# Placing SBUF tensors at 32-byte instead of 64-byte steps in a decoder-layer kernel

## Chip, cores and metric

The kernel runs on one core of a Trainium2 chip. The metric is the device time of one execution, in microseconds (us).

## What is computed

One decoder layer for 512 tokens of width 1024, and a final RMSNorm. In the reference's terms, cut:

```python
h = rmsnorm(x, norm1_g)
u_pool, q, k, v, qm, gate_logits = split(h @ w_in)
merged = (g0 * (pool_mixer(u_pool) @ w_branch_pool)      # causal pooling
        + g1 * (swa_with_sinks(q, k, v) @ w_branch_swa)  # window attention
        + g2 * (mem_attention(qm, mem) @ w_branch_mem))  # 256 memory tokens
x = x + merged @ w_out
h2 = rmsnorm(x, norm2_g)
# PEER: 8 heads pick 16 of 128*128 one-neuron experts per token
y = sum over picked experts of gate * gelu(h2 . u_e) * v_e
out = rmsnorm(x + y, final_norm_g)
```

## The kernel before

**Arithmetic.** TensorE works on fp32 data in three passes. Each operand is split into a high part (`_hi`, rounded to fp32r, a narrower float) and the remainder (`_lo`). A product is high times high, high times low and low times high, summed in PSUM.

**Weights.** All weights are one stream of 346 chunks of 128 x 1024 fp32 (512 KB). SP's queue loads a chunk into one of four `raw` buffers (line 264). ScalarE makes `w_hi` of it (line 761), GpSimd makes `w_lo` (line 415), both double-buffered, and TensorE uses the pair. TensorE reports `chunk_used`, on which ScalarE's next split waits.

**Stages.** In the projections, the expert scores and the gates of the branches, the weight chunk is the stationary operand and the moving one is `hT` (the normed tokens, transposed; line 438), a 128 x 512 operand. The branch projections take `yT` (branch outputs) as the moving operand instead (line 438 too). In the output projection and in the last stage, the values of the experts (line 635), the tokens are stationary (`mg` and `wT`, 128 x 128 at a time) and the weight chunk moves, 512 columns at a time. The stages follow each other: normalising and projecting (to about 280 us), gates and branches (to 500 us), output projection (to 519 us), queries and retrieval while expert scores run, then a stretch in which 64 expert chunks alternate with small bf16 matmuls on one-hot matrices `ohJ` and `ohI` (line 719, 907 to 1344 us), more expert scores, and from 1435 us on the value stage: 128 chunks of 24 matmuls. The last stage multiplies scores (`a_in`) by gates (`g_in`), both read back from HBM, into `wf` (VectorE, line 1356); ScalarE makes `wT_hi`, VectorE `wT_lo` (line 1360). Of `yT` there are 16 rows in a high and a low half, used for 8 output blocks. Of `mg` there are 8 rows, used for 4 token blocks and 2 column halves.

**Where the tensors lie.** One array `arena` of 212,800 bytes in each of the 128 partitions holds everything in SBUF. A `Place` hands out byte offsets in it in program order. The arena starts at byte 16,512 of a partition, which is 128 past a multiple of 512. `keep` holds what lives throughout: `x_sb`, `hT_hi`, `hT_lo`, `raw`, `w_hi`, `w_lo`, `subkeys`, `ident`, all of a multiple of 512 bytes each, and after them the small ones. Of those `gains` has 96 bytes, `pscale` 16, `sinks` 64, `freq` 8, `iota_b` 256, `iota_k` 64, `eps` 4, and eleven statistics arrays (`ssum` to `rinv`) 32 each. `front` is the offset after them. The other places start from it: `y` and `s`, then `a`, `g` and `p`, for the first half; `r`, and from `late` on `v`, for the second. Tensors of different stages share bytes. In these places the big tensors have multiples of 512 bytes; `gsm` has 128, and `ub`, `sA` and `sB` 2112 each.

```python
r = Place(front)
abuf = r("abuf", [2, T])
...
late = r.at
v = Place(late)
a_in = v("a_in", [4, T])
g_in = v("g_in", [2, BLOCKS, GROUP, STAGE_T])
wf = v("wf", [2, T])
wT_hi = v("wT_hi", [2, T], f32r)
wT_lo = v("wT_lo", [2, T], f32r)
```

Of the kernel before, what the change touches and what calls it, by code (L numbers as in the profile page):

```python
# [60 lines left out]
def build(nc, dram, out):  # L61
# [4 lines left out]
    with ExitStack() as ctx:  # L66
# [1 line left out]
        arena_size = 212800  # L68
        arena = ctx.enter_context(nc.sbuf_tensor("arena", [P, arena_size], mybir.dt.uint8))
        arena_at = int(nc.sbuf_base) - arena_size  # L70
        assert arena_at % 64 == 0

        class Place:

# [3 lines left out]
            def __call__(self, name, shape, dt=f32):  # L78
                t = nc.alloc_sbuf_tensor_at(name, [P] + list(shape), dt, offset=arena_at + self.at)
                size = int(np.prod(shape)) * (2 if dt == bf16 else 4)  # L80
                self.at += (size + 63) // 64 * 64
                assert self.at <= arena_size, (name, self.at)
                return t

# [1372 lines left out]
```

## Time and profile before

| | |
|---|---|
| median of 3 runs | 2138.91 us (2138.90 to 2138.99) |
| profiled execution, its own time | 2138.9 us |
| profiled execution, span of its instructions | 2137.1 us |
| TensorE busy | 2079.1 us, 97% of the span |
| VectorE, ScalarE, GpSimd busy | 57%, 37%, 40% |
| share of the 16 DMA engines, main queue | 45.0% |
| granted TensorE clock, mean | 0.988 of full |

The span runs from the first instruction to the last. The difference to the execution's own time, 1.8 us, lies around it. Busy times of matmuls overlap, since the profile gives each one from its start to a modelled end. So for TensorE the step from start to start is the cost of a matmul, and the timeline shows it.

### The profile page before, as it was taken

The numbers are of one execution on the slowest core, as the hardware profiler recorded it, in microseconds if no ns is written. First come the engines' busy times: TensorE is split into PE (matmuls) and PEld (weight loads), VectorE is DVE, ScalarE is ACT, GpSimd is POOL, SyncE is SP. The second block draws the span as 40 slices with busy tenths as digits, with TensorE's granted clock in tenths as the row PEclk, the third lists the DMA queues.
The fourth block names the chain that finished last, engine by engine and source line by source line (L and its number), as shares of the span: only waits on it lengthen the run. The fifth ranks groups of instructions, "written<-read, shape, count | busy, mean of one in ns | idle before, by whom it ended". The sixth has DMA issues, their size and how long they took to land.

```text
span 2137.1 us, 30302 instructions
## 1 busy us (share of the span) xinstructions
PE 2079.1 (97%) x10616; PEld 1712.0 (80%) x10616; DVE 1225.2 (57%) x1851; ACT 792.6 (37%) x1136; POOL 849.9 (40%) x361
## 2 busy tenths in 40 slices
PE   6979899999999999999999999999999999999998
PEld 5756788887888888888888888888888888888886
DVE  6688311113119999777777777015555555555556
ACT  5576422323223222355445544332222222222223
POOL 4411144444335544433333333444444444444443
PEclk9999999999999999999999999999999999999999
DMA  5211022222224545435665665665555555555552
GB/s 207 91 38 40 30 91 97 98 94 84 77 82 125 147 147 147 138 118 191 196 196 186 192 196 196 212 208 221 185 186 191 218 181 181 186 216 196 182 181 104
DMA packets 108516, 323.47 MB, mean 151 GB/s; under 512 B 11200, under 2 KB 11200, under 8 KB 106304
## 3 DMA queue, kind: packets, MB, share of 16 engines
q1 hardware_dynamic: 108192, 322.49, 45.0%
q10 hardware_dynamic: 288, 0.54, 0.1%
q8 instruction: 18, 0.29, 0.1%
q14 instruction: 18, 0.15, 0.0%
HBM read 253.78 MB, written 69.21 MB: 151 GB/s over the span
## 4 chain that ended last, share of the span: by engine, by line
issue 48%; PE 32%; POOL 19%; DMA 0%; POOLq 0%; DVE 0%; ACT 0%; SPq 0%
PE bank L635 32%; POOL w_lo L415 19%; DMA a_in<-a_rows 0%; POOLq L414 0%; DVE x_sb L1382 0%; POOLq L418 0%; DVE x_sb L1377 0%; POOL mask L401 0%; POOL mask L399 0%; DVE wf L1356 0%; DVE wT_lo L1360 0%; ACT wT_hi L992 0%; POOL mask L396 0%; POOL mask L404 0%; SPq L264 0%
## 5 line engine op out<-in xcount | busy, mean ns | idle before, releaser
L415 POOL TENSOR_TENSOR w_lo<-raw,w_hi 128x1024 fp32r<-128x1024 f32 x346 | 846.3, 2446 | 1268.4 <-ACT w_hi L761 1268.4
L761 ACT ACTIVATE w_hi<-raw 128x1024 fp32r<-128x1024 f32 x346 | 366.7, 1060 | 1219.4 <-PE bank L438 702.2
L438 PE MATMUL bank<-hT_hi,w_hi 128*128 128x512 f32 x1488 | 590.7, 397 | 0.8 <-POOL w_lo L415 0.4
L438 PE MATMUL bank<-hT_hi,w_lo 128*128 128x512 f32 x1488 | 580.3, 390 | 0.0
L438 PE MATMUL bank<-hT_lo,w_hi 128*128 128x512 f32 x1488 | 579.2, 389 | 0.0
L1360 DVE TENSOR_TENSOR wT_lo<-wf,wT_hi 128x512 fp32r<-128x512 f32 x128 | 313.1, 2446 | 131.2 <-ACT wT_hi L992 131.2
L438 PEld LDWEIGHTS bank<-hT_hi,w_lo 128*128 128x128 f32 x1488 | 279.3, 188 | 60.0
L438 PEld LDWEIGHTS bank<-hT_hi,w_hi 128*128 128x128 f32 x1488 | 279.6, 188 | 59.2 <-issue 4.1
L438 PEld LDWEIGHTS bank<-hT_lo,w_hi 128*128 128x128 f32 x1488 | 279.9, 188 | 56.0 <-issue 0.7
L635 PE MATMUL bank<-w_hi,wT_hi 128*128 128x512 f32 x1024 | 315.3, 389 | 0.1
L635 PE MATMUL bank<-w_lo,wT_hi 128*128 128x512 f32 x1024 | 315.2, 389 | 0.0
L635 PE MATMUL bank<-w_hi,wT_lo 128*128 128x512 f32 x1024 | 315.2, 389 | 0.0
L1356 DVE TENSOR_TENSOR wf<-a_in,g_in 128x512 f32<-128x512 f32 x128 | 89.1, 696 | 252.8 <-PE bank L635 160.6
L635 PEld LDWEIGHTS bank<-w_hi,wT_hi 128*128 128x128 f32 x1024 | 192.1, 188 | 40.4 <-DVE wT_lo L1360 0.6
L635 PEld LDWEIGHTS bank<-w_lo,wT_hi 128*128 128x128 f32 x1024 | 192.2, 188 | 39.9
L635 PEld LDWEIGHTS bank<-w_hi,wT_lo 128*128 128x128 f32 x1024 | 192.2, 188 | 39.9
L1334 DVE TENSOR_TENSOR ohJ<-iota_b,J 128x1024 bf16<-128x1024 bf16 x64 | 164.3, 2567 | 96.2 <-PE bank L719 96.2
L983 ACT ACTIVATE gstage<-bank 128x512 f32<-128x512 f32 x128 | 129.7, 1123 | 0.0
L1337 DVE TENSOR_TENSOR ohI<-eqI,G 128x1024 bf16<-128x1024 bf16 x192 | 121.4, 687 | 9.2
L1203 DVE TENSOR_TENSOR part<-sg,bank 128x512 f32<-128x512 f32 x24 | 15.1, 683 | 174.4 <-PE bank L438 174.4
L719 PEld LDWEIGHTS bank<-ohI,ohJ 128*128 128x128 bf16 x1536 | 85.9, 98 | 16.7 <-issue 16.7
L719 PE MATMUL bank<-ohI,ohJ 128*128 128x128 bf16 x1536 | 96.9, 219 | 0.0
(217 smaller groups left out, 1530.0 us busy)
## 6 DMA issues: line engine op xcount, KB each, us to landing
raw<-stream SPq DMA_DIRECT2D x346, 512.0 KB, 3.5
a_rows<-abuf SPq DMA_DIRECT2D x128, 256.0 KB, 4.0
g_rows<-gstage SPq DMA_DIRECT2D x32, 1024.0 KB, 6.1
g_in<-g_rows SPq DMA_DIRECT2D x16, 2048.0 KB, 9.4
a_in<-a_rows SPq DMA_DIRECT2D x128, 256.0 KB, 3.5
x_sb<-x SPq DMA_DIRECT2D x4, 512.0 KB, 8.9
out<-x_sb SPq DMA_DIRECT2D x4, 512.0 KB, 2.7
subkeys<-subkeys SPq DMA_DIRECT2D x1, 1024.0 KB, 14.2
```

The costliest lines, as they stand in the source:

```text
L415: pool.tensor_tensor(w_lo[:, k % 2, :], raw[:, k % RAW, :], w_hi[:, k % 2, :].bitcast(f32), ALU.subtract).then_inc(lo_ready, 1)
L438: last = pe.matmul(dst, w[:, slot, k * P:(k + 1) * P], rhs[low][:, r0 + k - k0, :], start=(k == k0 and wi == 0), stop=(k == k1 - 1 and wi ...
L635: last = pe.matmul(bank[2 * t + half][:, :], lhs[low_l][:, t * P:(t + 1) * P], w[:, slot, half * 512:(half + 1) * 512], start=first and lo ...
L719: last = pe.matmul(bank[2 + b][:, tk * P:(tk + 1) * P], ohJ[:, di, at, :], ohI[:, di, q, at, :], start=(q == 0), stop=(q == 2))
L761: act.activation(w_hi[:, base % 2, :], raw[:, slot, :], ACT.Copy).then_inc(hi_ready, 1)
L983: act.activation(gstage[:, half, :, t0:t0 + TOK_I // 2].rearrange("p i t -> p t i"), bank[2 + b][:, :].rearrange("p (t i) -> p t i", i=NKEYS),
L1203: dve.tensor_tensor(part[:, q, :], sg[:, q, :], bank[b][:, :], ALU.mult).then_inc(branch_read, 1)
L1334: dve.tensor_tensor(ohJ[:, di, :, :].rearrange(wide, e=2), ramp, over_keys(J2[:, toks, :]), ALU.is_equal)
L1337: last = dve.tensor_tensor(ohI[:, di, q, :, :].rearrange(wide, e=2), eqI[:, di, :, :].rearrange(wide, e=2), over_keys(G2[:, q, toks, :]), ...
L1356: dve.tensor_tensor(wf[:, di % 2, :].rearrange(tiles, b=BLOCKS), a_in[:, di % 4, :].rearrange(tiles, b=BLOCKS), g_in[:, di // GROUP, :, di ...
L1360: dve.tensor_tensor(wT_lo[:, di % 2, :], wf[:, di % 2, :], wT_hi[:, di % 2, :].bitcast(f32), ALU.subtract).then_inc(weighted_lo, 1)
```

## The change

Each tensor's size is rounded up to a multiple of 32 bytes instead of 64 before the next one is placed. The assertion on the arena's own start is relaxed likewise; the start itself stays where it is. No instruction, loop, semaphore or transfer is added, removed or reordered.

```diff
-        assert arena_at % 64 == 0
+        assert arena_at % 32 == 0
...
-                self.at += (size + 63) // 64 * 64
+                self.at += (size + 31) // 32 * 32
```

## Rows read from the trace of the kernel before

**Rows 1.** The page's first part: busy time, share of the span, instructions.

```profile
PE 2079.1 (97%) x10616; PEld 1712.0 (80%) x10616; DVE 1225.2 (57%) x1851; ACT 792.6 (37%) x1136; POOL 849.9 (40%) x361
```

**Rows 2.** Windows: from:to, length, busy us by engine, PEclk, DMA share, GB/s.

```profile
962.00:1344.00 382.00, 382.00 (x2672) 317.68 (x2671) 278.34 (x271) 192.83 (x223) 133.44 (x56) 1.00 0.59 191
1454.00:2110.00 656.00, 656.00 (x2896) 543.17 (x2894) 381.45 (x241) 190.04 (x240) 290.04 (x121) 1.00 0.53 188
```

**Rows 3.** The same view, TensorE alone, a stretch early in the kernel.

```profile
45.20:46.40 1.20, 1.20 (x4) 0.50 0.00 0
```

**Rows 4.** Groups by line and shape: busy us, mean ns of one, idle before.

```profile
L438 PE MATMUL bank<-hT_hi,w_lo 128*128 128x512 f32 x1488 | 580.3, 390 | 0.0
...
L635 PE MATMUL bank<-w_hi,wT_lo 128*128 128x512 f32 x1024 | 315.2, 389 | 0.0
...
L635 PEld LDWEIGHTS bank<-w_hi,wT_lo 128*128 128x128 f32 x1024 | 192.2, 188 | 39.9
...
L1337 DVE TENSOR_TENSOR ohI<-eqI,G 128x1024 bf16<-128x1024 bf16 x192 | 121.4, 687 | 9.2
...
L438 PE MATMUL bank<-yT_hi,w_lo 128*128 128x512 f32 x128 | 50.6, 395 | 0.0
...
L635 PE MATMUL bank<-w_hi,mg_hi 128*128 128x512 f32 x64 | 20.2, 395 | 0.0
```

**Rows 5.** Timeline, TensorE, value stage: start us, us; first and last of 13.

```profile
1599.32 0.61 PE L635 MATMUL bank<-w_hi,wT_hi 128*128 128x512 f32 x2
...
1604.76 0.61 PE L635 MATMUL bank<-w_hi,wT_hi 128*128 128x512 f32 x2
```

**Rows 6.** Timeline, TensorE, branch projection going over to a gate projection.

```profile
340.07 0.40 PE L438 MATMUL bank<-yT_hi,w_hi 128*128 128x512 f32 x1
...
342.87 0.39 PE L438 MATMUL bank<-hT_hi,w_hi 128*128 128x512 f32 x1
...
345.61 0.39 PE L438 MATMUL bank<-hT_hi,w_hi 128*128 128x512 f32 x1
...
346.97 0.39 PE L438 MATMUL bank<-hT_hi,w_hi 128*128 128x512 f32 x1
```

**Rows 7.** Timeline, TensorE, output projection; first and last of four pairs.

```profile
505.70 0.63 PE L635 MATMUL bank<-w_hi,mg_hi 128*128 128x512 f32 x2
...
507.10 0.63 PE L635 MATMUL bank<-w_hi,mg_hi 128*128 128x512 f32 x2
```

**Rows 8.** Timeline, TensorE, early stretch; first and last of four.

```profile
45.23 0.63 PE L492 MATMUL bank<-w_lo,memT_hi 128*128 128x512 f32 x1
...
46.51 0.47 PE L492 MATMUL bank<-w_lo,memT_hi 128*128 128x512 f32 x1
```

**Rows 9.** Timeline, TensorE, expert chunk behind bf16 matmuls; first and last of ten.

```profile
1012.50 0.39 PE L438 MATMUL bank<-hT_lo,w_hi 128*128 128x512 f32 x1
...
1014.59 0.39 PE L438 MATMUL bank<-hT_lo,w_hi 128*128 128x512 f32 x1
```

**Rows 10.** One line's instructions: count, ns min/median/max, first and last start.

```profile
L1108 DVE TENSOR_TENSOR sA<-sB x4: 691/692/693, 79.3 to 93.9; 128x512 f32<-128x512 f32 x4
```

**Rows 11.** The same view by tile: what touches `top`.

```profile
L1248 DVE MAX8 top<-cand x64: 274/280/298, 641.0 to 821.6; 128x8 f32<-128x128 f32 x64
...
L1255 DVE MAX8 top<-cand x64: 273/276/297, 652.8 to 833.4; 128x8 f32<-128x128 f32 x64
```

**Rows 12.** The same view by tile: what touches `ohJ`.

```profile
L719 PE MATMUL bank<-ohI,ohJ x1536: 219/219/230, 907.5 to 1343.0; 128*128 128x128 bf16 x192
```

**Rows 13.** Waits from 1400 us on: total us, times, longest.

```profile
DVE wf L1356 <- PE bank L635: 160.6, 118, 1.9
...
DVE wf L1356 <- DMA a_in<-a_rows: 92.2, 8, 77.3
```

**Rows 14.** The chain that ended last, around 1440 us: start, us, what.

```profile
1439.87 10.27 DMA a_in<-a_rows
...
1452.31 674.87 PE bank L635 x2976
```

## The prediction

> **What bounds the kernel now.** I read the first part of the page, then the windows: TensorE is busy for 97% of the span [rows 1], and in the long stretches all of the time, 656 of 656 us in the value stage and 382 of 382 in the gate stretch, at full clock [rows 2]. The chain that ended last is TensorE alone for its last 675 us [rows 14]. So the time is the number of matmuls times the step from one start to the next, and whatever the change does elsewhere counts only if it stretches those steps or opens gaps. VectorE has room in the value stage: it waits for TensorE 118 times, 1.36 us on average [rows 13].
>
> The groups by shape then show something that bears on placement: matmuls of one shape don't all last alike. Those on `hT` and `wT` take 389 to 390 ns, those on `yT` and `mg` 395 [rows 4]. Those are modelled ends, so I read starts. In the value stage 24 matmuls take 1604.76 − 1599.32 = 5.44 us, 226.7 ns each [rows 5]. On `yT`, 12 take 342.87 − 340.07 = 2.80 us, 233.3 each; on `hT` soon after, 6 take 346.97 − 345.61 = 1.36 us, 226.7 each [rows 6]. On `mg`, 6 take 1.40 us, 233.3 [rows 7].
>
> **What the change moves.** Fifteen small tensors lose 32 bytes each in `keep`: `gains` (96 instead of 128), `pscale`, `freq`, `eps` and the eleven statistics (32 instead of 64). `front` falls by 15 × 32 = 480 bytes. In what follows it every size is a multiple of 64 already, so all of it shifts by the same 480. The tensors before `gains` stay. Places modulo 512, from the arena's start and the sizes in the kernel's description:
>
> - `hT`, `raw`, `w_hi`, `w_lo`, `ident`: 128, unchanged.
> - `yT`, `mg`, `memT`, `abuf` (at `front` or whole multiples of 512 behind it): before 0, now −480, that is 32.
> - `ohJ`, `ohI`, `a_in`, `g_in`, `wf`, `wT` (128 further, for `gsm`): before 128, now 160.
>
> So the two operands of a matmul lie like this. `hT` with `w`: 128 and 128 before and after. `wT` with `w`: 128 and 128 before, 160 and 128 now. `yT` or `mg` with `w`: 0 and 128 before, 32 and 128 now.
>
> **Cost by part.**
>
> Instructions, transfers, waits: none added or removed, 0.
>
> TensorE on `hT`: unchanged, 0. It is the largest share (3 × 1488 of 10616).
>
> TensorE on `wT`: 3 × 1024 = 3072 matmuls, nothing covers them, and each ns of step costs 3.07 us. Before, the two kinds of pair that share their place modulo 512 ran at 226.7, the two that differ by 128 bytes at 233.3. That is a correlation over two distances (0 and 128), and no row has a distance of 32. From above the nearest row is 233.3: 3072 × 6.6 ns = +20.3 us. From below it is the stretch at half clock (granted 0.50, 1.2 GHz) [rows 3]: 3 matmuls of this shape take 46.51 − 45.23 = 1.28 us, 427 ns each [rows 8]. Half of that, 213.3 ns, would be a step at 2.4 GHz without anything extra: 3072 × −13.4 = −41.2 us. In between, a linear share 32/128 of 6.6 ns is 1.65 ns or +5.1 us. I take 0: the modulus is the nearest to the one seen fast, and in the expert chunks the step comes back to 226.7 from 232.2 after a break (1014.59 − 1012.50 over 9 matmuls, operands at the same places) [rows 9]. So that step is something that the stream settles into, and I expect 32 bytes not to push it out.
>
> TensorE on `yT` (3 × 128), `mg` (3 × 64) and 48 on `memT` as the stationary operand: 624 matmuls at 233.3, whose distance falls from 128 to 96. No row has 96. If they fell to 226.7: 624 × 6.6 = −4.1 us. If they rose as much again, +4.1. I take 0.
>
> TensorE on one-hots: 1536 small matmuls, both operands move together, 0. From the first to the last of 64 passes go 1343.0 − 907.5 = 435.5 us [rows 12], 6.91 for each of 63, of which 24 expert matmuls take 5.44 and 24 small ones the rest, 61 ns each. At 3% more (233.3 over 226.7) that would be 2.8 us.
>
> The Trainium skill (TensorE: Matmul & The Clock Gate, Back-to-back issue gap) puts a warm step of 512 columns at N/2.4 + 2.5 = 215.8 ns, and says nothing of the operands' addresses. The trace does not agree, 226.7 at best. By that page's figure the value stage would have an estimated 3072 × 10.9 = 33 us to give back, if new places freed it from the extra.
>
> Weight loads of `wT`: 188 ns [rows 4] under a step of 226.7, so 38.7 ns of cover. If a row of 128 values at an odd place took an eighth longer, 212 ns, it would still be covered. By more than a fifth it would show.
>
> VectorE and ScalarE: `sA <- sB` reads its source shifted by 4 to 32 bytes against the destination (shifts of 2 to 16 tokens are built from steps of 1, 2, 4 and 8 fp32 values) and takes 692 ns, 691 to 693 [rows 10]: the shift does not show in it. MAX8 writes its first eight values at a multiple of 64 from the tensor's start and the second eight 32 bytes on, at 280 and 276 ns [rows 11]. I take 0 for all of VectorE; the two engines are not on the path anyway. What it costs if that is wrong for bf16 stands under the rivals.
>
> Transfers: `abuf`, `a_in`, `g_in`, `gstage` move by 32 bytes modulo 512; chunk loads don't. The value stage uses 0.53 of the DMA engines [rows 2]. One transfer is on the path: at 1439.87 an `a_in` block lands after 10.27 us and VectorE, ScalarE and TensorE follow at 1452.31 [rows 14]. A 32-byte piece more in a row of 2048 bytes, 1 in 64, makes that 0.16 us. I take 0, at most +0.2.
>
> The Trainium skill (DMA: Bandwidth & Descriptors, How a descriptor splits into AXI transactions) says that a transfer is cut at multiples of 256 bytes and that a start off such a multiple costs extra beats of 32. No row here shows beats. By it the moved tensors, at 128 modulo 256 or 0 before, would read one beat more per row, an estimated 65 for 64: the same 0.16 us.
>
> Sum: the profiled execution's 2138.9 us (span 2137.1 and 1.8 around it) + 0 = 2138.9, and the median of the runs is 2138.91.
>
> **Rivals.**
>
> *The value stage takes the slower step.* Decides at: the `wT` and `w` operands no longer at the same place modulo 512. For it: both pairs at unlike places are slow, both at like ones fast, whether the tokens move (`yT`) or stand (`mg`). Against it: 128 bytes are four times 32. Price +20.3: 2159.2 us. A weaker form at the linear share gives 2144.0.
>
> *The value stage gets faster.* The step of 226.7 holds 13.4 ns more than half of the cold one, so there is something to lose. Against it: no row at full clock is near 213. Half of it back: −20.6, 2118.3 us.
>
> *Branch and output projections fall to 226.7 and nothing else moves*: 2134.8 us.
>
> *VectorE's bf16 operations lose a fast form.* `ohI` takes 687 ns for 1024 elements [rows 4], fp32 692 for 512 [rows 10]. At one element's pace that would be 1384, so four operations in a pass (`eqI`, three `ohI`) get 2.8 us longer. The window of 382 us holds 55.3 passes of 6.91 us, and VectorE is idle for (382 − 278.34)/55.3 = 1.87 us of each [rows 2]. Exposed 0.9 × 64 = 58 us: 2197. Against it: 160 is still a multiple of 32, and shifts of 4 bytes cost fp32 nothing.
>
> **How the numbers follow.** Under 0.2% (4.3 us) a measurement of this kernel hardly tells from no change. Nothing moves: 0.38. Only the branch and output projections fall (2134.8, still within 0.2%): 0.08. Value stage at 233.3: 0.25; at the linear share: 0.08. bf16 form lost: 0.05. Value stage faster: 0.16, spread down to 2097. Together: faster 0.16, same 0.46, slower 0.38. The likeliest is no change, 2138.9, its own range 2134.8 to 2140. The range over the cases: below 2128 lies some 0.10, above 2161 some 0.08, so 2128 to 2161.
>
> **What would show it.** Right: timeline rows of the value stage with 24 matmuls in 5.44 us, `yT` and `mg` at 233.3, `hT` at 226.7, the groups' means of `L635` and `L1337` at 389 and 687 ns, the wait for `a_in` at 10.3 us. Wrong: `wT` matmuls at 395 ns mean and 5.60 us per chunk, or 5.2 and below; VectorE's `ohI` over 1 us with TensorE waiting for it; a weight load over 188 ns. What would make it wrong is that two read streams of TensorE disturb each other by their distance, and that 32 bytes of distance are enough.

## The result and the profile after

The changed kernel takes 2159.01 us (median of 4 runs, 2158.59 to 2160.14) where the kernel before takes 2138.9. The ratio is 1.0099, 95% interval 1.0087 to 1.0110: slower by 20 us. The forecast was no change, 2138.9. The measured time is inside the stated range, and within 0.2 us of the first rival's 2159.2.

The instructions are the same 30302, and TensorE is still busy for 97% of the span. The page's first part, of after:

```profile
span 2158.0 us, 30302 instructions
...
PE 2096.3 (97%) x10616; PEld 1709.1 (79%) x10616; DVE 1226.7 (57%) x1851; ACT 792.1 (37%) x1136; POOL 850.9 (39%) x361
```

The instructions that touch `wT_hi` show where the time went: of one kind of value-stage matmul, the duration and the starts of the first and last. First before, then after.

```profile
L635 PE MATMUL bank<-w_hi,wT_hi x1024: 389/389/497, 1430.2 to 2125.9; 128*128 128x512 f32 x171
```

```profile
L635 PE MATMUL bank<-w_hi,wT_hi x1024: 392/395/504, 1430.9 to 2146.8; 128*128 128x512 f32 x171
```

The last starts 695.7 us behind the first before and 715.9 after: +20.2. Up to the first, the kernel has lost 0.7 us in the profiled pair. There are 3067 steps between the two, so 226.8 ns a step before and 233.4 after. TensorE is hardly idle in between: one spot has steps of 534 and 335 ns before and of 358 and 342 after. What comes after the stage takes the same 10.3 us in both.

The timeline of after, TensorE, in the value stage, answers to [rows 5]:

```profile
1596.32 0.63 PE L635 MATMUL bank<-w_hi,wT_hi 128*128 128x512 f32 x2
...
1601.92 0.63 PE L635 MATMUL bank<-w_hi,wT_hi 128*128 128x512 f32 x2
```

That is 24 matmuls in 5.60 us, 233.3 ns each, where it was 5.44 us. The branch projection and the gate projection behind it, to be set beside [rows 6]:

```profile
337.94 0.39 PE L438 MATMUL bank<-yT_hi,w_hi 128*128 128x512 f32 x1
...
342.16 0.39 PE L438 MATMUL bank<-hT_hi,w_hi 128*128 128x512 f32 x1
...
344.92 0.39 PE L438 MATMUL bank<-hT_hi,w_hi 128*128 128x512 f32 x1
...
347.64 0.39 PE L438 MATMUL bank<-hT_hi,w_hi 128*128 128x512 f32 x1
```

On `yT` 18 matmuls take 4.22 us, 234.4 ns each (233.3 before). The first 12 on `hT` behind them take 2.76 us, 230.0 each, as the stream settles (2.74 before); the next 12 take 2.72 us, 226.7 each, as before. The output projection, beside [rows 7]:

```profile
500.26 0.63 PE L635 MATMUL bank<-w_lo,mg_hi 128*128 128x512 f32 x2
...
503.06 0.63 PE L635 MATMUL bank<-w_lo,mg_hi 128*128 128x512 f32 x2
```

That is 12 matmuls in 2.80 us, 233.3 ns each, unchanged. (By its first and last matmul this stage runs from 480.5 to 525 us in the kernel before, and the value stage starts at 1430.2; the description of the stages puts them at 500 to 519 and at 1435.) The groups by shape and the single lines of after that answer to [rows 4, 10 to 12]:

```profile
L635 PE MATMUL bank<-w_hi,wT_lo 128*128 128x512 f32 x1024 | 321.3, 396 | 0.0
L635 PEld LDWEIGHTS bank<-w_hi,wT_lo 128*128 128x128 f32 x1024 | 192.5, 188 | 46.4
L1337 DVE TENSOR_TENSOR ohI<-eqI,G 128x1024 bf16<-128x1024 bf16 x192 | 121.3, 686 | 9.2
...
L1108 DVE TENSOR_TENSOR sA<-sB x4: 691/691/694, 79.5 to 94.1; 128x512 f32<-128x512 f32 x4
...
L1255 DVE MAX8 top<-cand x64: 274/276/296, 653.0 to 833.6; 128x8 f32<-128x128 f32 x64
...
L719 PE MATMUL bank<-ohI,ohJ x1536: 219/219/229, 907.7 to 1343.7; 128*128 128x128 bf16 x192
```

VectorE's operations, the weight loads and the one-hot matmuls last what they did. The matmuls on `wT` are longer, 396 ns instead of 389; those on `yT` are longer by 1 ns a step, and all others are as they were.

Other engines are not what slows these matmuls. The windows view of after, all engines, with the starts of TensorE in that stretch:

```profile
1793.85:1795.25 1.40, 1.40 (x8) 1.13 (x7) 0.00 (x0) 0.00 (x0) 0.00 (x0) 1.00 0.63 129
```

```profile
1793.72 0.63 PE L635 MATMUL bank<-w_hi,wT_hi 128*128 128x512 f32 x2
...
1795.12 0.63 PE L635 MATMUL bank<-w_hi,wT_hi 128*128 128x512 f32 x2
```

VectorE, ScalarE and GpSimd do nothing there, and 6 matmuls still take 1.40 us, 233.3 ns each. Over the value stage the 456 steps with all three idle average 233.3 ns and the 243 with all three busy 233.3. In the kernel before both averages are 226.7. The 979 steps of after during which no DMA engine moved anything average 233.4 ns, the others 233.3.

### The profile page after: what moved, and what is told of

It reads as the page before. It is cut to its first block, busy times and chain, and to the rows that moved or that the text cites. A ratio compares the mean times of both kernels' runs of the same rounds, so it can differ in the third digit from the quotient of the medians.

```text
span 2158.0 us, 30302 instructions
## 1 busy us (share of the span) xinstructions
PE 2096.3 (97%) x10616; PEld 1709.1 (79%) x10616; DVE 1226.7 (57%) x1851; ACT 792.1 (37%) x1136; POOL 850.9 (39%) x361
## 4 chain that ended last, share of the span: by engine, by line
PE 68%; issue 23%; POOL 9%; DVE 0%; POOLq 0%
PE bank L635 33%; PE bank L438 30%; POOL w_lo L415 9%; PE bank L719 4%; DVE x_sb L1382 0%; POOLq L414 0%; POOLq L418 0%; PE bank L703 0%; DVE x_sb L1377 0%; POOL mask L401 0%; POOL mask L399 0%; POOL mask L396 0%; POOL mask L404 0%; DVE rstd L1381 0%; POOL ident L394 0%
## 5 line engine op out<-in xcount | busy, mean ns | idle before, releaser
L635 PE MATMUL bank<-w_hi,wT_hi 128*128 128x512 f32 x1024 | 321.4, 396 | 0.0
L635 PE MATMUL bank<-w_lo,wT_hi 128*128 128x512 f32 x1024 | 321.3, 396 | 0.0
L635 PE MATMUL bank<-w_hi,wT_lo 128*128 128x512 f32 x1024 | 321.3, 396 | 0.0
```

Source lines behind the costliest of these rows:

```text
L635: last = pe.matmul(bank[2 * t + half][:, :], lhs[low_l][:, t * P:(t + 1) * P], w[:, slot, half * 512:(half + 1) * 512], start=first and lo ...
```

## The experiments

Theories. D: the step depends on the distance between the places of the two operands. B: an operand off a multiple of 64 bytes is read more slowly by itself. R: the loss comes from the other moved tensors. Places are counted from the start of the arena that the description gives; no run prints it, and the distances don't depend on it. Steps below are worked out from the starts in each trace.

**1. Move `wT` alone.** On the kernel before:

```diff
+        v.at += 32
         wT_hi = v("wT_hi", [2, T], f32r)
```

> The kernel before with wT alone placed 32 bytes further (160 modulo 512, w at 128); all else at its old place. Theory D (the step of a matmul depends on the distance between the places of its two operands): the value stage goes to 233.3 ns a matmul, some 20.3 us more, 2159 us. Rival R (the loss comes from the other moved tensors, a_in, g_in, the one-hots): 2139 us with wT matmuls at 226.7 ns. Rival B (an operand that does not start at a multiple of 64 bytes is read more slowly, whatever the other one's place): 2159 us too; this run does not tell D from B.

2157.03 us against 2137.46 for the kernel before on the same chip, ratio 1.0091 (1.0076 to 1.0107).

```profile
L636 PE MATMUL bank<-w_hi,wT_hi x1024: 392/395/498, 1428.6 to 2144.5; 128*128 128x512 f32 x171
```

715.9 us from first to last, the changed kernel's number. R falls.

**2. Move all but `wT`.** On the changed kernel:

```diff
+        v.at += 480
         wT_hi = v("wT_hi", [2, T], f32r)
```

> The changed kernel with wT alone put back to 128 modulo 512 (480 bytes of padding ahead of it); all other tensors at their new places. Theories D and B: 2139 us, the value stage back at 5.44 us a chunk. Rival R: 2159 us.

2138.67 us, ratio to the kernel before 1.0006 (0.9997 to 1.0016): within 0.2%. First to last 695.6 us:

```profile
L636 PE MATMUL bank<-w_hi,wT_hi x1024: 389/389/497, 1431.3 to 2126.9; 128*128 128x512 f32 x171
```

So `wT` is the whole of the loss, as far as this can be measured.

**3. Move everything by 32 bytes.** On the kernel before:

```diff
-        keep = Place(0)
+        keep = Place(32)
```

> The kernel before with everything in SBUF, w and hT too, placed 32 bytes further, so that every distance between two tensors is as before and no big tensor starts at a multiple of 64. Theory D: no change, 2139 us, hT and wT matmuls at 226.7 ns, yT and mg at 233.3. Rival B: the value stage at 233.3 ns or more (+20 us) and the matmuls on hT too (4464 times up to 6.6 ns, +29 us), so 2160 to 2190 us.

2137.56 us, ratio 1.0001 (0.9991 to 1.0010).

```profile
L635 PE MATMUL bank<-w_hi,wT_hi x1024: 389/389/497, 1428.9 to 2124.5; 128*128 128x512 f32 x171
...
L635 PE MATMUL bank<-w_hi,mg_hi x64: 392/394/398, 478.5 to 522.1; 128*128 128x512 f32 x64
```

Here `wT` lies at 160 modulo 512 as in the changed kernel, and is read at the fast step, because `w` lies at 160 too. B falls and D stands: the start of a tensor by itself costs nothing, its distance from the other operand does.

**4. All at the place of `w`.** On the kernel before, `yT`, `mg` and `memT` to 128 modulo 512, `wT` staying there:

```diff
-        front = keep.at
+        front = keep.at + 128
...
+        r.at += 384
         late = r.at
```

> The kernel before with yT, mg and memT placed 128 bytes further, so that they lie at 128 modulo 512 like w and hT; wT stays at 128. Theory D: branch and output projections go from 233.3 to 226.7 ns a matmul, 624 times 6.6 ns, 4.1 us less: 2134.8 us. Rival B: no change, 2139 us, since all were at multiples of 64 already.

2133.99 us, ratio 0.9983 (0.9974 to 0.9992): 3.5 us faster than the kernel before on the same chip (2137.46). The expected 4.1 us lie inside the interval, which reaches from 1.7 to 5.6 us.

```profile
L439 PE MATMUL bank<-yT_hi,w_hi x128: 389/389/389, 275.9 to 476.5; 128*128 128x512 f32 x128
...
L636 PE MATMUL bank<-w_hi,mg_hi x64: 389/389/389, 477.1 to 519.5; 128*128 128x512 f32 x64
```

The output projection runs from 477.1 to 519.5, 42.4 us, where it took 524.1 − 480.5 = 43.6 in the kernel before. Of the 192 matmuls, 187 steps lie between those two starts: 226.7 ns each, and 233.2 before.

**5 to 9. A map of distances.** Five kernels on top of the kernel before, each with its own padding ahead of `hT`, `yT`, `mg` and `wT`, and made up for behind it so that `w` stays at 128. The first of them:

```diff
+        keep.at += 256
         hT_hi = keep("hT_hi", [KC, T], f32r)
         hT_lo = keep("hT_lo", [KC, T], f32r)
+        keep.at += 256
...
-        front = keep.at
+        front = keep.at + 192
...
-        g = Place(y.at)
+        g = Place(y.at + 192)
...
+        r.at += 320
         late = r.at
...
+        v.at += 64
         wT_hi = v("wT_hi", [2, T], f32r)
```

> Distances of the operand that isn't w from w, in bytes modulo 512: wT 64, yT 64, mg 256, hT 256. Theory D1 (any distance but 0 modulo 512 gives the slow step): wT, yT, mg and hT all at 233.3 ns, so 20.3 us for wT and 4464 times some 6 ns, 26 us, for hT more than before, 2185 us. Rival D2 (the pattern repeats every 256 bytes): hT and mg at 226.7, wT and yT at 233.3, 2158 us. Rival D3 (the step rises with the distance up to 128): wT at 230.

> Distances from w, in bytes modulo 512: wT 128, yT 256, mg 32, hT 32. D1: all at 233.3 ns, 2185 us. D2: yT at 226.7, the others at 233.3, 2183 us. D3: hT and mg below 233, wT at 233.3.

> Distances from w, in bytes modulo 512: wT 256, yT 32, mg 64, hT 480 (that is 32 bytes ahead of w instead of behind). D1: all at 233.3 ns, 2185 us. D2: wT at 226.7, so 2165 us. If the sign counts, hT at 480 differs from hT at 32 in the run before.

> Distances from w, in bytes modulo 256: wT 192, yT 192, mg 96, hT 64. Theory D2 (fast only where the distance is a multiple of 256): all above 226.7 ns. From the runs so far wT and mg (stationary) 232 to 233.3, hT at 64 as yT was at 64 in the first map, 229.2, or 233.3 as at 32. Rival D4 (some other distance is faster than 0): a step under 226. Time some 2160 to 2175 us.

> Distances from w, in bytes modulo 256: wT 224, yT 96, mg 192, hT 192. D2: all above 226.7 ns, wT as at 32, 233.3. D4: a step under 226. Time some 2165 to 2175 us.

They took 2156.91, 2173.5, 2158.94, 2152.82 and 2179.22 us (before on the same chips 2137.72 for the first three, 2138.0 for the other two). Windows of TensorE in the five, in that order: a stretch of `hT` and one of `wT`. With TensorE always busy, length over count is nearly the step; the count takes in a matmul or two that began ahead of the window, so it comes out up to 0.7 ns low in the shorter one.

```profile
710.00:870.00 160.00, 160.00 (x706) 1.00 0.48 143
1460.00:2100.00 640.00, 640.00 (x2744) 1.00 0.51 186
```

```profile
710.00:870.00 160.00, 160.00 (x687) 1.00 0.47 139
1460.00:2100.00 640.00, 640.00 (x2755) 1.00 0.52 190
```

```profile
710.00:870.00 160.00, 160.00 (x687) 1.00 0.47 140
1460.00:2100.00 640.00, 639.73 (x2823) 1.00 0.54 195
```

```profile
710.00:870.00 160.00, 160.00 (x701) 1.00 0.49 143
1460.00:2100.00 640.00, 640.00 (x2798) 1.00 0.53 189
```

```profile
710.00:870.00 160.00, 160.00 (x686) 1.00 0.46 138
1460.00:2100.00 640.00, 640.00 (x2744) 1.00 0.54 190
```

The counts 706 and 2823, the fast step (160/706 = 227 ns), stand where `hT` or `wT` was 256 bytes off `w`. The counts 686, 687 and 2744, the slow step (233 ns), stand at 32, 192 and 480 bytes behind `w` for `hT` and at 64 and 224 for `wT`. At 128, `wT` has 2755 (232 ns). In between lie 701 and 2798 (228 to 229 ns), at 64 for `hT` and 192 for `wT`.

The signs make sense once the distance is written as start of the moving operand less start of the stationary one, modulo 256. `hT` and `yT` move while `w` stands; `wT` and `mg` stand while `w` moves. The mean step in ns, worked out from the starts, with the run that shows it in brackets:

| distance | tokens move (`hT`, `yT`) | tokens stand (`wT`, `mg`) |
|---|---|---|
| 0 | 226.7 (`yT`, 4) | 226.7 (`wT`, 7), 226.9 (`mg`, 5) |
| 32 | 233.3 (`hT`, 6) | 233.3 (`wT`, 9) |
| 64 | 228.9 (`hT`, 8), 229.2 (`yT`, 5) | 228.9 (`wT`, 8; `mg`, 9) |
| 96 | 233.6 (`yT`, 9) | 233.4 (`mg`, after) |
| 128 | 233.2 (`yT`, before) | 233.3 (`mg`, before), 232.4 (`wT`, 6) |
| 160 | 234.2 (`yT`, after) | 234.2 (`mg`, 8) |
| 192 | 233.4 (`hT`, 9) | 233.3 (`wT`, 5) |
| 224 | 233.3 (`hT`, 7) | 233.3 (`wT`, after) |

Both roles give one curve. It repeats every 256 bytes (D2). Four pairs of the map that the table leaves out are within 0.2 ns of their rows. The fifth, `yT` at 256 bytes in the sixth run, averages 227.4: behind the slow `hT` stretch the first seven steps of each block average 231.7, and from the eighth on they are 226.7. So the step needs some matmuls to settle, as in [rows 9]. Theory D1, a period of 512, falls, and so does D3, a rise with the distance: at 32 the full price is there already. No distance tried beats 0, so D4 falls for multiples of 32.

The expected times of the eighth and ninth run were missed: 2152.82 us lies below 2160 to 2175, since `wT` at 192 bytes behind `w` had 228.9 ns and not 232 or more, and 2179.22 lies above 2165 to 2175.

The fifth run came out as D2 had it, 2156.91 us against 2158. For the sixth both expected sums, 2185 (D1) and 2183 (D2), were too high, and so was D2's 2165 for the seventh, both with a slow `hT`. In the sixth run, 6.6 ns on 4464 `hT` matmuls would be 29 us, and the value stage started only 17.8 us later (1448.0 instead of 1430.2). The starts of the stages show where the rest is. The projections before the first branch block gained 2.6 us instead of losing 2.8. `yT` got faster by 2.2. And in the one-hot stretch 64 chunks lost 6.8 us instead of 10, because their matmuls were not at the fast step before. Timeline of before:

```profile
1010.87 1.51 PE L719 MATMUL bank<-ohI,ohJ 128*128 128x128 bf16 x24
1012.19 0.47 PE L438 MATMUL bank<-hT_hi,w_hi 128*128 128x512 f32 x1
...
1017.76 1.51 PE L719 MATMUL bank<-ohI,ohJ 128*128 128x128 bf16 x24
```

The 24 expert matmuls take 5.57 us there, 232.1 ns each, the first step being longer and the next ones not yet settled; the 24 small ones take 1.32 us, 55 ns each. A pass took 6.91 us and takes (1358.3 − 916.0)/63 = 7.02 in the sixth run. The first projections end 2.0 us sooner in the third run too, where no distance changed, so their 2.6 us are within what varies from run to run.

**10 and 11. Half a weight load.** In the value stage each stationary operand gets 64 of its 128 tokens, so the results for the other 64 are left out. On the kernel before and on the changed one:

```diff
-                            last = pe.matmul(bank[2 * t + half][:, :], lhs[low_l][:, t * P:(t + 1) * P],
+                            last = pe.matmul(bank[2 * t + half][0:width, :], lhs[low_l][:, t * P:t * P + width],
```

with `width` 64 in the value stage and 128 elsewhere.

> The kernel before, but in the value stage each stationary operand has only the first 64 of its 128 tokens, so the results for the other 64 of every 128 tokens are left out. Same number of matmuls, each still moves 512 columns; each weight load reads half. wT at distance 0. Theory L (the nanoseconds above 213.3 come from the weight load's reads beside those of the moving operand): they halve, 13.4 to some 7, a step of 220 ns, 20 us less, 2118 us. Rival M (they belong to the moving operand alone): 226.7 ns, 2138 us.

> The same edit on the changed kernel, wT at distance 32; the results for 64 of every 128 tokens are left out again. Theory L: the 20 ns above 213.3 halve, a step of some 223 ns, 31 us less than the changed kernel, 2127 us. Rival M: 233.3 ns, 2158 us.

2147.55 and 2154.29 us. One kind of matmul and its load in the tenth and in the eleventh run:

```profile
L635 PEld LDWEIGHTS bank<-w_hi,wT_hi x1024: 132/135/136, 1428.5 to 2134.2; 128*64 128x64 f32 x171
L635 PE MATMUL bank<-w_hi,wT_hi x1024: 389/395/441, 1428.7 to 2134.4; 128*64 128x512 f32 x171
```

```profile
L635 PEld LDWEIGHTS bank<-w_hi,wT_hi x1024: 133/134/136, 1431.1 to 2141.8; 128*64 128x64 f32 x171
L635 PE MATMUL bank<-w_hi,wT_hi x1024: 392/397/450, 1431.3 to 2142.0; 128*64 128x512 f32 x171
```

The load falls from 188 to 134 ns. The step goes to 705.7/3067 = 230.1 ns at distance 0, which is slower than with the whole load, and to 710.7/3067 = 231.7 at distance 32 bytes of `wT`, faster than with it. Neither theory L (220 and 223) nor rival M (226.7 and 233.3) holds as it was put. The step does change with the width of the stationary operand, so it doesn't belong to the moving operand alone. But less reading can cost more, so it isn't a price per byte read either. How the two streams of reads fall together in time seems to matter; that is argued, not shown, and the edit also narrows the output. The mechanism behind the dependence on the distance stays open.

**12. The changed packing with like places.** On the changed kernel:

```diff
-        front = keep.at
+        front = keep.at + 96
...
+        r.at += 128
         late = r.at
```

> The changed kernel, tensors still packed at 32 bytes, with 96 bytes of padding ahead of front and 128 ahead of late, so that yT, mg and memT lie at 128 modulo 512 and wT at 384, all at distances from w that are multiples of 256. Theory D2: hT, yT, mg and wT all at 226.7 ns: the 2134 us of the version of the kernel before with all like, 24 us less than the changed kernel. If the changed packing cost something besides, it would stay above that, 2139 or more.

2133.88 us against 2137.72 for the kernel before on the same chip, ratio 0.9985 (0.9975 to 0.9995). `wT` is at 384 here, 256 off `w`:

```profile
L636 PE MATMUL bank<-w_hi,wT_hi x1024: 389/389/496, 1424.0 to 2119.7; 128*128 128x512 f32 x171
```

So 32-byte packing costs nothing of itself. This version and the fourth are 0.15 and 0.17% faster than the kernel before, which both intervals just tell from no change.

## Why the prediction was wrong

- **What bounds the kernel: right.** Matmuls times step gave the time. 3072 times the measured 6.6 ns is 20.3 us; the value stage grew by 20.2.
- **Which pairs change: right.** `hT` stayed at 226.7 ns and `wT` moved against `w`.
- **TensorE on `wT`, "I take 0": the step that failed.** The term was 0 and measured +20.2 us, which is its own upper bound, +20.3. The reason given was that 32 bytes are nearest to the distance seen fast. That took it for granted that the step rises smoothly with distance. The map shows the full 233.3 at 32 bytes, less at 64, and full again at 96. The two pairs of points in the trace [rows 5 to 7] said that distance matters and nothing about how; the modulus of 512 that I read into them is 256.
- **"Something that the stream settles into" [rows 9]: seen, but no support for 0.** The changed kernel settles too, in the value stage on steps of 232.5 and 234.2 ns in turn. Where a stream settles is what the distance sets.
- **The rival "the value stage takes the slower step": right** in place, mechanism and price, 2159.2 against 2159.01. It had 0.25 where no change anywhere had 0.38, against two rows that spoke for it and only a guess about smoothness against it.
- **`yT`, `mg`, `memT`, "I take 0": nearly right.** `yT` went from 233.2 to 234.2 ns (384 times 1.0, +0.4 us), `mg` stayed. The −4.1 us that I named for 226.7 is there to be had: the fourth run measured −3.5.
- **Weight loads, VectorE, one-hots: right at 0.** 188 ns, `ohI` 686 ns, MAX8 276 ns, one-hot pass (1343.7 − 907.7)/63 = 6.92 us. The reading of that pass was off: not 5.44 us of expert matmuls and 61 ns for each small one, but 5.57 us and 55 ns, as the fence above shows.
- **Transfers: right at 0, and there was little on the path to lose.** The median landing of an `a_in` block is 3.5 us before and after, that of an `abuf` block 4.0. The 10.27 us landing [rows 14] held TensorE up by one step of 534 ns, some 0.3 us. It is no longer in the chain, which around 1440 us is TensorE alone:

```profile
1434.78 25.43 PE bank L635 x108
```

A landing of 10.0 to 10.3 us is in the chain in every run whose `wT` step is 230.1 ns or less (the second to fourth, seventh, eighth, tenth and twelfth), and in none with 231.7 or more (the first, fifth, sixth, ninth and eleventh). That fits a block which arrives in time when the steps are slower; it was not tested by itself.

- **Faster value stage: wrong.** No distance at a multiple of 32 bytes got under a mean of 226.7, in any of the 14 profiled kernels.

The Trainium skill (SBUF — State Buffer, Who interferes with whom) gives TensorE two independent read ports, one for the moving operand and one for weight loads, and says that "PE and ACT never wait on anyone". The trace agrees on other engines: the steps are alike with them idle and busy, 233.3 ns in after and 226.7 before. But TensorE's two streams are not free of each other: moving one operand by 32 bytes changed the step by 6.6 ns (first run), moving both together by nothing (third). The measurement decides.

## What to carry to other kernels

Where TensorE is the bound and streams fp32 operands at full clock, compare the step from start to start across operand pairs of one shape; a difference of 3% between pairs is worth a look at their addresses. In this kernel it paid to place the big matmul operands a multiple of 256 bytes from each other, whatever the packing of the small tensors around them; a rounding of small sizes can shift all that follows. Only fp32 operands, with a new weight load for every matmul, were tried. And where two points show an effect and its shape is unknown, don't draw a straight line between them.

## What was not expected of the hardware

- The step depends on one number, moving start less stationary start modulo 256 bytes: 226.7 ns at 0 once settled, 229 at 64, 232.4 to 234.2 at the other multiples of 32, alike in both roles.
- The extra is not there at half clock: at 1.2 GHz the step is 427 ns [rows 8], twice 213.3, with operands 128 bytes apart, a distance that costs 233 ns at 2.4 GHz. In the ninth run, with `memT` at distance 160 and a granted clock of 0.50, 6 steps take 48.75 − 46.19 = 2.56 us, 427 ns each; in the twelfth, at distance 0 and the same clock, 3 take 1.28 us, 427 ns too. The lines are those of the ninth run:

```profile
46.19 0.63 PE L496 MATMUL bank<-w_lo,memT_hi 128*128 128x512 f32 x1
...
48.75 0.63 PE L496 MATMUL bank<-w_lo,memT_hi 128*128 128x512 f32 x1
```

- At full clock even the best distance keeps 13.4 ns above 213.3, and halving the weight load at that distance makes it 16.8.
